# Moving the multiplications of the fourth modulation from GpSimd to ScalarE, and delaying the casts of a convolution tile by one unit, in a two-network kernel

## What is computed

```python
h = rms_norm(x, norm_pre[l, 1])
p = h @ c_w_in[o]                      # 1024 -> 3 * 1024
gate_b, gate_c, xt = p[..., :1024], p[..., 1024:2048], p[..., 2048:]
mix = (gate_b * causal_depthwise_conv(gate_c * xt, c_conv_w[o])) @ c_w_out[o]
x = x + rms_norm(mix, norm_post[l, 1])
```

```python
c_act = jax.nn.silu(c)
mod = c_act @ mod_w[layer] + mod_b[layer]   # 1024 -> 6 * 1024, for two layers
```

## Time and profile before

| what | value |
|---|---|
| median of 3 runs | 2760.32 us |
| the profiled execution's own time | 2777.21 us |
| its span, first to last instruction | 2775.3 us |
| busy: TensorE, VectorE, ScalarE, GpSimd | 94%, 79%, 53%, 34% |
| mean granted TensorE clock | 0.959 |
| convolution block, first matmul to the end of its projection | 755.5 to 869.6 us |
| GpSimd at work on the fourth group | 757.2 to 936.8 us |

### The profile page before, as it was taken

One profiled execution on the slowest core, in us unless ns is written; L12 is line 12 of the kernel. 1 busy time (PEld: TensorE's weight loads), 2 busy tenths in 40 slices (PEclk: granted clock), 3 DMA queues, 4 the chain that ended last, 5 costly groups with the idle time before them and its releaser, 6 DMA issues. The chain is left out here.

```text
span 2775.3 us, 47290 instructions
## 1 busy us (share of the span) xinstructions
PE 2610.2 (94%) x17706; PEld 2387.6 (86%) x17706; DVE 2181.2 (79%) x2487; ACT 1481.3 (53%) x1930; POOL 935.8 (34%) x586
## 2 busy tenths in 40 slices
PE   7999899999997998978998977999999999999997
PEld 7999699999996998758998846999999999999986
DVE  6678666767787685987855996898989898989888
ACT  4337543533434334424334514777777777777765
POOL 6980089688699991125900130000000000000000
PEclk9999899999898998999999987999999999999998
DMA  8764267577565553324554414999999899999985
GB/s 298 256 234 153 97 239 259 194 259 254 201 218 209 207 183 137 128 94 162 187 181 144 160 60 156 353 344 334 348 336 349 340 346 340 348 341 349 342 314 211
DMA packets 129208, 670.57 MB, mean 242 GB/s; under 512 B 14672, under 2 KB 14992, under 8 KB 80064
## 3 DMA queue, kind: packets, MB, share of 16 engines
q1 hardware_dynamic: 111024, 604.72, 59.4%
q0 software_dynamic: 18064, 64.21, 6.8%
HBM read 667.82 MB, written 1.05 MB: 241 GB/s over the span
## 5 line engine op out<-in xcount | busy, mean ns | idle before, releaser
L1713 PE MATMUL work<-xT_hi,wh_gu 128*128 128x256 f32 x2088 | 600.9, 288 | 27.1 <-DVE xT_lo L979 11.9
L1714 PE MATMUL work<-xT_lo,wh_gu 128*128 128x256 f32 x2088 | 599.0, 287 | 0.0
L1715 PE MATMUL work<-xT_hi,wl_gu 128*128 128x256 f32 x2088 | 598.4, 287 | 0.0
L1713 PE MATMUL work<-wh_gu,mixT_hi 128*128 128x256 f32 x1792 | 510.2, 285 | 4.3 <-DVE mixT_lo L1426 3.0
L1714 PE MATMUL work<-wl_gu,mixT_hi 128*128 128x256 f32 x1792 | 508.3, 284 | 0.0
L1715 PE MATMUL work<-wh_gu,mixT_lo 128*128 128x256 f32 x1792 | 507.8, 283 | 0.0
L856 DVE TENSOR_TENSOR wl_gu<-raw_gu,wh_gu 128x2048 fp32r<-128x2048 f32 x158 | 388.7, 2460 | 81.5 <-ACT wh_gu L394 80.9
L1713 PEld LDWEIGHTS work<-xT_hi,wh_gu 128*128 128x128 f32 x2088 | 408.3, 196 | 36.5 <-issue 28.7
L1714 PEld LDWEIGHTS work<-xT_lo,wh_gu 128*128 128x128 f32 x2088 | 408.6, 196 | 4.8
L1715 PEld LDWEIGHTS work<-xT_hi,wl_gu 128*128 128x128 f32 x2088 | 408.1, 195 | 0.0
L861 DVE TENSOR_TENSOR wl_d<-raw_d,wh_d 128x1024 fp32r<-128x1024 f32 x157 | 245.4, 1563 | 177.3 <-ACT wh_d L401 177.3
(11 more groups left out here) (431 smaller groups left out, 4818.8 us busy)
## 6 DMA issues: line engine op xcount, KB each, us to landing
raw_gu<-in_w_gu SPq DMA_DIRECT2D x271, 1024.0 KB, 5.3
raw_d<-in_w_d SPq DMA_DIRECT2D x269, 512.0 KB, 5.2
scratch<-in_w_gu SPq DMA_DIRECT2D x112, 1024.0 KB, 7.1
scratch<-in_w_d SPq DMA_DIRECT2D x112, 512.0 KB, 7.7
scratch<-in_w_mod POOLq DMA_DIRECT2D x96, 512.0 KB, 3.7
scratch<-in_s_b POOLq DMA_DIRECT2D x16, 256.0 KB, 3.0
rows<-in_norm_post POOLq DMA_DIRECT2D x6, 512.0 KB, 4.3
rows<-in_ln_g POOLq DMA_DIRECT2D x4, 512.0 KB, 5.2
```

Source lines behind the costliest of these rows:

```text
L1713: pe.matmul(out_, w[0], m[0], start=start, stop=False)
L1714: pe.matmul(out_, w[0], m[1], start=False, stop=False)
L1715: return pe.matmul(out_, w[1], m[0], start=False, stop=stop)
```

## The change

In the convolution block ScalarE now does the 24 multiplications of the fourth group, three in each of its eight steps: one behind the casts of unit n + 1 and two behind the copy of xt (Copy with a column of c_act as scale). Each signals mod_scaled. GpSimd issues the loads and does the 21 adds. The casts of a finished tile, mix_hi on ScalarE and mix_lo on VectorE, move from step n to the end of step n + 1. Buffers, sums and loads are the same; the first three groups are unchanged.

```diff
 # ScalarE, cmix
+                def scaled(m):
+                    dst = MACC[3][m // 8] if m % 8 == 0 else MW[m % 3]
+                    act.wait_ge(mod_in[m % 3], 16 * (8 * 3 + m // 3 + 1))
+                    act.activation(dst, MW[m % 3], ACT.Copy, scale=c_act[:, m % 8:m % 8 + 1]).then_inc(mod_scaled, 1)
+
+                def mixed(n):
+                    act.wait_ge(c_y, n + 1)
+                    mix_hi(MH[:, n, :], CY[n % 2])
+
                 for n in range(8):
                     hi(U + n + 1)
+                    scaled(3 * n)
                     act.wait_ge(d_used, U + n + 1)
                     act.activation(CXT[n % 2], c_bank(n, 2), ACT.Copy).then_inc(c_x, 1)
-                    act.wait_ge(c_y, n + 1)
-                    mix_hi(MH[:, n, :], CY[n % 2])
+                    scaled(3 * n + 1)
+                    scaled(3 * n + 2)
+                    if n:
+                        mixed(n - 1)
+                mixed(7)
 # VectorE, cmix
+                def mixed(n):
+                    mix_lo(ML[:, n, :], CY[n % 2], MH[:, n, :])
...
                     TT(CY[k], CY[k], gate_b, ALU.mult).then_inc(c_y, 1)
-                    mix_lo(ML[:, n, :], CY[k], MH[:, n, :])
+                    if n:
+                        mixed(n - 1)
+                mixed(7)
 # GpSimd
+            def last_modulation():
+
+                pool.wait_ge(xt_l, 4 * (MOD_AT[3] + 1))
+
+                def load(n):
+                    m = n - 3
+                    if m >= 0 and m % 8 == 0:
+                        pool.wait_ge(mod_scaled, m + 1)
+                    elif m >= 0:
+                        pool.wait_ge(mod_term, 72 + m - m // 8)
+                    pool.dma_start(MW[n % 3], A["w_mod"][72 + n]).then_inc(mod_in[n % 3], 16)
+
+                for n in range(3):
+                    load(n)
+                for n in range(24):
+                    acc = MACC[3][n // 8]
+                    if n % 8:
+                        pool.wait_ge(mod_scaled, n + 1)
+                        if n % 8 > 1:
+                            pool.wait_ge(mod_term, 72 + n - 1 - (n - 1) // 8)
+                        TT(acc, acc, MW[n % 3], ALU.add).then_inc(mod_term, 1)
+                    if n + 3 < 24:
+                        load(n + 3)
+                pool.wait_ge(mod_term, 72 + 21)
+                pool.memset(small[:, 7:8], 0.0).then_inc(mod_sums, 1)
...
-                    if b in MOD_AT:
+                    if b in MOD_AT[0:3]:
                         modulation(MOD_AT.index(b))
+                    if b == MOD_AT[3]:
+                        last_modulation()
```

More of the change, by code:

```diff
@@ L236, in program @@
         mod_in = [sem(f"mod_in{i}") for i in range(3)]
+        mod_scaled = sem("mod_scaled")
         mod_term, mod_sums, mod_cols, mod_copied = (sem("mod_" + n) for n in ("term", "sums", "cols", "copied"))
```

## The result

The changed kernel takes **2781.86 us** (median of 5 runs, 2780.76 to 2785.31), the kernel before, run beside it, 2765.79 us (median of 5, 2758.7 to 2767.61). The ratio is 1.0063, 95% interval 1.0047 to 1.0079: slower by 16.1 us. The profiled execution of after took 2781.12 us, span 2779.3 us. The forecast was 2770.4 us, slower by 10.1: of the 11.5 us between, 5.5 are the base (2760.3 from three runs, 2765.8 from five) and 6.0 the size.

The account below looks back on a forecast made before the run. The prediction took a loop over the engines with VectorE in it twice, held by GpSimd's adds, to set the convolution block's pace. +12.0 for the units and -1.9 behind gave +10.1 on 2760.3: 2770.4 us, range 2750 to 2786.

Parts of the forecast that it names:

- case A: Convolution block: GpSimd's adds and VectorE share one resource, which is full; 2770.4 us, range 2763 to 2779, chance 0.58.
- The price of an add: Convolution block's units: each GpSimd add holds one VectorE operation, 2.06 us each, bounds 0 and 2.5.
- The stretch: Convolution block's units, first product to projection: 89.3 us by VectorE's work, 21 adds and 2 idle, in place of 78.5.
- the walk: Convolution block, engines' lists followed step by step from 755.5 us: VectorE rounds of 12.5 to 12.9 us, together +13.3.
- VectorE's groups some 50 us over price: Convolution block: VectorE's L861, L1085 and taps take in sum near 50 us more than their unhindered price.
- Rival C: Convolution block: adds slip beside VectorE's PSUM products and into gaps, TensorE sets the pace; 2744 us, chance 0.17.
- Behind the block, -1.9: After the convolution block: GpSimd silent, so the second residual operation falls from 3.18 to 1.28 us; bounds 0 and -3.
- rival D: Convolution block: GpSimd multiplications held VectorE for all 2.85 us, so 31 us go and 23 come; 2749 us, chance 0.05.
- The ring: Convolution block: ScalarE's multiplication, casts, low part, add, wait and landing form a loop of 12.3 us, cost by itself 0.
- Rival B: Convolution block: three buffers decide, each landing taking 5.2 us, loop 13.9 us; 2782 us, chance 0.12.
- ScalarE's multiplications at 0: Convolution block: ScalarE's 24 multiplications, 3.1 us per step, hide where 5.4 us of waiting were; cost 0.
- +10.8 us: Convolution block's units: lengthening by the sum, 89.3 in place of 78.5 us; the forecast took the middle, +12.0.

## Why the prediction was right, and what was mis-sized

**The direction and case A** held. The time of 2781.9 lies in the range (2750 to 2786), but 3 us above A's own (to 2779).

**The price of an add, 2.06 us: right.** VectorE's busy time in the stretch less its own 44.0 us is 43.8 us; by 21 adds that is 2.09 each. **The stretch** was 89.3 us by the sum, 91.8 by the walk and 90.5 by the middle that the forecast took: 90.3 measured. Idle left to VectorE: 2 forecast, 2.5 found. **Units every 12 to 13 us:** on average yes (low parts of 2048 columns from 767.13 to 840.63, six intervals of 12.25), singly from 7.6 to 17.2. The even round of the walk does not exist. **Projection near 858:** 853.1, since all began some 4.6 us earlier.

**VectorE's groups some 50 us over price:** in the groups that were named (here L876, L1100 and the three taps) it is 40, and 4.7 more stand in the low parts of 2048 columns (L871), which were not named. The forecast's own 21 x 2.06 gives 43, so the 50 did not follow from it. **The c_y waits gone but for the last: right. TensorE's waits for low parts over 15 us:** 13.7, a little less; the wait ahead of the projection grew by 3.

**Rival C, the adds slip beside:** it needed an add below 1.6 us, and they cost 2.09. How things would stand below it the short adds show, 2755.7 us.

**Behind the block, -1.9: right.** Mark to b = 5's first matmul was 14.6 us and is 12.6; both residual operations take 1.3. b = 5's own units did not change.

**Multiplications off GpSimd, 0.4 each, and rival D:** in the kernel whose adds became multiplications, a GpSimd multiplication of 2.85 us costs VectorE 0.4 us on average, and its low part of 1024 columns takes 1.22. The Trainium skill (SBUF — State Buffer, Who interferes with whom) says, of VectorE's 2-port modes, that whoever issues first gets the pair of ports shared with GpSimd for the whole instruction. The adds here hold VectorE for about their whole length (2.09 of 2.4 us), though the tap of 778.27 starts 0.18 us before its add by the profile and is held all the same; the multiplications do not hold it so.

**The ring, "as long as VectorE's round" (12.3 against 12.9), priced at 0: right for this kernel,** where three more buffers change nothing (2782.3). But I had it for a matter of landings at 5.2 us only, and it is a second limit of nearly the same height. Take the adds' hold on VectorE away and the time stays (2785.0, with a GpSimd operation 0.6 us longer on average; how high the ring stands with the add's own length no run shows by itself). Take the ring away and VectorE gives the same time. Rival B's number, 2782, was met to the microsecond, but the six buffers rule out its reason; that is chance.

**ScalarE's multiplications at 0: right only beside the later casts.** Without these the change costs 24.0 us, not 16.1 (2791.6 against 2767.6 beside it).

**The term that was mis-sized** is the base of "+10.8 us", and with it the last line of the sum, "the profiled execution, 2777.21 us, would become 2787.3". The 78.5 us for the stretch were those of one execution; two more had a block of 120.4 and 120.3 us instead of 127.5, and the stretch, read in one of them, took 74.0. None of the timed runs of the kernel before on record took longer than 2771.8 us. Worked against the repeated execution, VectorE's own work is 66.58 less 22.7 us over price in L861, L1085 and two taps, 43.9, as before; plus 21 x 2.06 + 2 it is 89.2, that is +15.2, and -1.9 gives +13.3, against 14.2 in the traces and 16.1 timed. I had seen that the profiled execution stood 16.9 us above the median of the runs and carried the whole distance over as if it lay outside the block; 7 of it lay inside. The remaining 3 us are no more than what the untouched rest of the program differs by between two executions: b = 9 took 1074.8 and 1078.0 us in the two repeats.

## What to carry to other kernels

Price an add on GpSimd by what it takes from VectorE, and ask in which stretch VectorE has that time to give: 21 adds of full length cost 26 us in this block, and in the sub-block behind it they and 18 multiplications together 5. Where two limits stand at nearly the same height, one experiment against each is not enough: each alone says "no effect", and only both together show what is to be had. And when the profiled execution lies well above the median of the runs, look where the distance lies before using a length of it as the base of a difference.

## What was not expected of the hardware

- GpSimd's multiplication and its add are treated unlike by VectorE's operations. An add gets in between two queued VectorE operations and then holds the next one for nearly its whole 2.4 us (778.27 above). A multiplication beside two queued ones waits for both: 5.06 us instead of 2.85 at 801.60 in the kernel before, repeated (L1644), and 4.71 at 780.40 above. Once running, it does not hold VectorE for its whole length: in the kernel with multiplications for adds most of VectorE's operations keep their time, and the others take 0.3 to 1.35 us longer.
- The same block of one kernel takes 120.3, 120.4 or 127.5 us. Where in the adds' order VectorE's operations happen to fall may decide it: both short executions have the steady 8.75-us rhythm, the long one has not. That was not tested by itself.
- The loads of the modulation's blocks land later where DMA is busier, though its share is not all: median 3.6 us after the issue before (DMA busy 0.59 of the stretch), 4.2 in the changed kernel (0.69), 4.7 with multiplications for adds (0.68), 5.8 with the short adds (0.90).
